# Sample gates in the third mLSTM chunk, their squares one chunk later, and sigmoids ended on ScalarE by Ln and Exp

## What is computed

```
h = _head_rms(jax.nn.sigmoid(_to_heads(o_ml, ML_HEADS)) * h, ml_g)
...
o_h = _head_rms(o_h, hg_g) * jax.nn.silu(_to_heads(hgt, HG_HEADS))
...
mixed = jnp.concatenate([_from_heads(h), _from_heads(o_h)], axis=-1).astype(x.dtype)
out = jnp.einsum('bte,ed->btd', mixed, w_out)
```

## Time and profile before

| | us |
|---|---|
| median of 3 runs | 1206.72 |
| lowest and highest | 1206.54, 1207.07 |
| profiled execution, its own time | 1207.56 |
| its span in the trace | 1205.4 |

### The profile page before, as it was taken

The page is one execution under the profiler, slowest core; times in us unless marked ns, Lnnn a source line. Parts: engine busy times, 40 slices in busy tenths (PEclk is TensorE's granted clock), DMA queues, the critical chain, the costliest instruction groups (busy, mean ns, idle before and its releaser), DMA issues.

```text
span 1205.4 us, 17280 instructions
## 1 busy us (share of the span) xinstructions
PE 1013.3 (84%) x6738; PEld 605.7 (50%) x6738; DVE 600.5 (50%) x1007; ACT 249.1 (21%) x532; POOL 249.1 (21%) x228
## 2 busy tenths in 40 slices
PE   7999999979999696999999999734878899799400
PEld 4666666645656364566656665423434445344100
DVE  1550133347777777797778777362222233231046
ACT  1542111121111122233223322100011111011023
POOL 0000000001110142453344334000000001252165
PEclk9999999989999897999999999855999999899755
DMA  9010101020000243000010001409887779858496
GB/s 386 29 70 1 70 1 70 0 74 1 1 1 1 79 181 158 19 18 18 36 36 18 18 36 53 164 19 369 337 292 289 279 286 339 324 210 318 123 218 179
DMA packets 30681, 154.29 MB, mean 128 GB/s; under 512 B 5546, under 2 KB 5994, under 8 KB 21274
## 3 DMA queue, kind: packets, MB, share of 16 engines
q1 hardware_dynamic: 24938, 130.17, 28.5%
q0 software_dynamic: 5248, 18.94, 6.1%
q10 hardware_dynamic: 432, 4.35, 0.9%
HBM read 321.52 MB, written 23.82 MB: 286 GB/s over the span
## 4 chain that ended last, share of the span: by engine, by line
PE 76%; DMA 11%; DVE 7%; issue 2%; POOL 1%; ACT 1%; SPq 1%; DVEq 0%; ACTq 0%; POOLq 0%
PE psum L1653 17%; PE psum L774 9%; PE psum L1704 9%; PE psum L761 9%; DMA hg_decay<-in_w_up 6%; PE psum L1333 5%; PE psum L1312 4%; PE psum L1328 4%; PE psum L802 4%; DMA x_cm<-y_slots,hg_k 2%; PE psum L736 1%; PE psum L1671 1%; PE psum L1297 1%; POOL x_cm L1423 1%; DMA hg_q<-in_w_down 1%
## 5 line engine op out<-in xcount | busy, mean ns | idle before, releaser
L1653 PE MATMUL psum<-x_cm,weight_slots 128*128 128x344 f32 x720 | 209.0, 453 | 0.0
L1653 PEld LDWEIGHTS psum<-x_cm,weight_slots 128*128 128x128 f32 x720 | 136.6, 190 | 71.9 <-issue 1.1
L1704 PE MATMUL psum<-weight_slots,x_cm 128*128 128x512 f32 x256 | 114.0, 599 | 0.0
L1328 PE MATMUL psum<-weight_slots,scratch 128*32 128x256 f32 x1280 | 80.1, 406 | 23.1 <-DMA weight_slots<-in_w_gate 16.9
L1408 POOL DMA_INDIRECT scratch<-x_rows,hg_k x20 | 19.8, 991 | 307.4 <-PE psum L1297 222.0
L1312 PE MATMUL psum<-conv_qk,scratch 128*32 128x512 f32 x320 | 74.1, 605 | 10.9 <-DMA hg_q<-in_w_down 6.6
L1333 PE MATMUL psum<-conv_qk,scratch 128*32 128x256 f32 x640 | 74.1, 385 | 7.4 <-DMA hg_decay<-in_w_up 7.4
L1704 PEld LDWEIGHTS psum<-weight_slots,x_cm 128*128 128x128 f32 x256 | 48.1, 193 | 54.5 <-issue 54.5
L1333 PE MATMUL psum<-hg_decay,scratch 128*32 128x256 f32 x640 | 74.1, 385 | 0.0
L1312 PE MATMUL psum<-hg_k,scratch 128*32 128x512 f32 x160 | 74.0, 606 | 0.0
L1312 PE MATMUL psum<-hg_q,scratch 128*32 128x512 f32 x160 | 74.0, 606 | 0.0
(11 more groups left out here) (356 smaller groups left out, 1679.5 us busy)
## 6 DMA issues: line engine op xcount, KB each, us to landing
weight_slots<-in_w_gate SPq DMA_DIRECT2D x80, 1024.0 KB
conv_qk<-in_w_up SPq DMA_DIRECT2D x40, 1024.0 KB
hg_decay<-in_w_up SPq DMA_DIRECT2D x40, 1024.0 KB
conv_qk<-in_w_down SPq DMA_DIRECT2D x40, 1024.0 KB
hg_k<-in_w_down SPq DMA_DIRECT2D x20, 1024.0 KB
hg_q<-in_w_down SPq DMA_DIRECT2D x20, 1024.0 KB
weight_slots<-in_w_in SPq DMA_DIRECT2D x6, 2048.0 KB, 7.7
y_slots<-scratch SPq DMA_DIRECT2D x20, 512.0 KB, 7.2
```

Of the source, the lines that this page charges most:

```text
L1328: m = mm(PS[lane, 2, 0:FF], xgT[i][:, k, lane], w_gate[q][:, k], start=(k == 0), stop=(k == KD - 1))
L1653: i = mm(PS[0:m, idx % 4, 0:PIECE], lhs_of(k), xT[:, k, n * PIECE:(n + 1) * PIECE], start=(k == 0), stop=(k == KD - 1))
L1704: i = mm(PS[:, bank, :], xT[:, k, c * P:(c + 1) * P], w_slot(g)[:, k, :], start=(k == 0), stop=(k == KD - 1))
```

## The change

Three things change, and buffers move with them.

1. **Sigmoids.** ACT ends both chunk gates and the samples' gates itself: `exp(-x)`, then `Ln` with a bias of 1, then `Exp` with scale -1, so 1/(1+exp(-x)). The add and the reciprocal on DVE are gone (L1976 and L1977; L1154 and L1155; L674 and L675). In the mLSTM chunk DVE's wait for `o_exp` moves from before the memory update to before the last multiplication.
2. **The samples' gates** run on DVE in the mLSTM chunk c = 2, between the score step and the v step, and not behind the last chunk's output. The two clearing memsets are done by POOL: one behind the mask copy at the start, one behind its last square of the mLSTM loop. The store of the samples' stabiliser (`out_m_s`) moves on SP from stage 3 to between the store of the memory and the load of weight group 7.
3. **The samples' squares** are summed on PE in chunk 1 behind its first level, the root follows on ACT behind `outputs_scale(0)`, `samples_mix` moves from level 2 to 3, the samples' output projection on PE from level 1 to 2, their residual sum on DVE and its root on ACT one level later. Since `squares` now lies in the place of `ln_gb`, SP waits for the sum of squares before it loads `ln_gb`, and the samples' rows of x behind it.

```
-    T = [SC[:, 5632 + n * HB:5632 + (n + 1) * HB] for n in range(24)]
-    squares, both_rstd = SC[:, 6400:6400 + 2 * HB], SC[:, 6464:6464 + 2 * HB]
-    TH = {m: SC[:, 6528 + n * HB:6528 + (n + 1) * HB] for n, m in enumerate((0, 2, 11, 15))}
+    tile32 = lambda at, n=0: SC[:, at + n * HB:at + (n + 1) * HB]
+    squares, both_rstd = SC[:, 8832:8832 + 2 * HB], SC[:, 5696:5696 + 2 * HB]
+    q_dots, decay_args = SC[:, 9216:9216 + 2 * HB], SC[:, 9280:9280 + 3 * HB]
+    T = {0: q_dots[:, 0:HB], 1: q_dots[:, HB:], 8: tile32(9280), 9: tile32(9312), 10: tile32(9344), 6: tile32(9376), 7: tile32(9408),
+         16: tile32(8704), 17: tile32(8736), 15: tile32(5632)}
+    TH = {0: tile32(8768), 2: tile32(8800), 15: tile32(5664), 11: conv_ps[:, 0:HB]}
     T[5], TH[5], T[13], TH[13] = squares[:, 0:HB], squares[:, HB:], both_rstd[:, 0:HB], both_rstd[:, HB:]
-    T[21] = mprev.rearrange("p h c -> p (h c)")[:, 0:HB]
+    T[21] = tile32(9440)
...
+    T[11] = T[12]
...
-    q_apart = [SC[:, 7680:8704], SC[:, 8704:9728]]
+    q_apart = [SC[:, 7680:8704], SC[:, 5632:6656]]
...
         store_v_rows(1)
         sp.wait_ge(s.num_rows, 2)
         sp.dma_start(w_out, t["w_out"].rearrange("(e p) n -> p e n", p=P)).then_inc(s.mixer_in, 16)
-        sp.wait_ge(s.masks_made, 1)
         sp.wait_ge(s.h_turned_read, NCH)
+        sp.wait_ge(s.sq_sum, 1)
+        sp.wait_ge(s.outputs, 16 * outs[0])
         sp.dma_start(ln_gb, t["ln1"].partition_broadcast(P)).then_inc(s.mixer_in, 16)
...
-                out_dma(sp, t["out_m_s"].rearrange("h b -> (h b)").unsqueeze(0), T[21][0:1])
...
@@ -640,11 +644,9 @@
         link(v.tensor_tensor(hb(dec), mb, hb(T[6]), ALU.subtract))
         link(v.tensor_tensor(hb(T[21]), hb(T[6]), lf, ALU.add))
         tell(v.tensor_scalar(nm, T[21], -1.0, None, ALU.mult), s.sgates_arg)
-        dve.wait_ge(s.masks_made, 1)
-        for q in q_apart:
-            link(v.memset(q, 0.0))
         dve.wait_ge(s.qk_silu, 9)
         qs, ks = conv_ps[:, 0:HB], conv_ps[:, HB:2 * HB]
+        dve.wait_ge(s.masks_made, 2)
         link(v.tensor_copy(spread_q(0), hb(qs)))
         link(v.tensor_tensor(T[0], qs, ks, ALU.mult))
         tell(v.tensor_tensor(T[1], qs, n0, ALU.mult), s.dots_in)
@@ -658,6 +660,7 @@
         link(v.tensor_tensor(hb(TH[0]), qS, kS, ALU.mult))
         dve.wait_ge(s.sgates_exp, 2)
         link(v.tensor_tensor(hb(TH[2]), qS, hb(TH[14]), ALU.mult))
+        dve.wait_ge(s.masks_made, 3)
         tell(v.tensor_copy(spread_q(1), hb(TH[2])), s.dots_in)
         link(v.tensor_scalar(dd, dd, KSCALE, None, ALU.mult))
         link(v.tensor_tensor(T[3], ks, dd, ALU.mult))
@@ -668,13 +671,9 @@
 
     def samples_gate(dve, link, kind):
 
-        v = nc.vector
-        gate = (T, TH)[kind][11]
         dve.wait_ge(s.ogate_exp, kind + 1)
-        link(v.tensor_scalar(gate, gate, 1.0, None, ALU.add))
-        link(v.reciprocal(gate, gate))
         if kind == 1:
-            link(v.tensor_tensor(TH[11], TH[11], TH[12], ALU.mult))
+            link(nc.vector.tensor_tensor(TH[11], TH[11], TH[12], ALU.mult))
...
-                    if l == 7:
-                        samples_squares(pe)
-                if c == 1 and l == 1:
+                if c == 1 and l == 0:
+                    samples_squares(pe)
+                if c == 1 and l == 2:
                     project_out_samples()
...
         def gate_exp(kind):
             act.wait_ge(s.zs_read, kind + 1)
-            tell(A((T, TH)[kind][11], (T, TH)[kind][12], ACT.Exp, scale=-1.0), s.ogate_exp)
+            gate = (T, TH)[kind][11]
+            link(A(gate, (T, TH)[kind][12], ACT.Exp, scale=-1.0))
+            link(A(gate, gate, ACT.Ln, bias=one_col))
+            tell(A(gate, gate, ACT.Exp, scale=-1.0), s.ogate_exp)
...
+            if c == 1:
+                norm_scale()
...
-                if l == (3 if c == 1 else 2) and c >= 1:
+                if l == (4 if c == 1 else 2) and c >= 1:
                     ln_scale(ROW_ORDER[c - 1])
...
-                    tell(A(PS[:, 1, :], gtb.rearrange("p h v -> p (h v)"), ACT.Exp, scale=-1.0), s.gt_exp)
+                    link(A(PS[:, 1, :], gtb.rearrange("p h v -> p (h v)"), ACT.Exp, scale=-1.0))
+                    link(A(PS[:, 1, :], PS[:, 1, :], ACT.Ln, bias=one_col))
+                    tell(A(PS[:, 1, :], PS[:, 1, :], ACT.Exp, scale=-1.0), s.gt_exp)
...
-            if c == 0:
-                norm_scale()
...
-                if c == 1 and l == 2:
+                if c == 1 and l == 3:
                     samples_mix(dve, link, tell, 0)
                     samples_mix(dve, link, tell, 1)
-                if l == 2 + late and c >= 1:
+                if l == 2 + 2 * late and c >= 1:
                     residual_sum(ROW_ORDER[c - 1])
...
                     dve.wait_ge(s.gt_exp, c + 1)
-                    link(v.tensor_scalar(PS[:, 1, :], PS[:, 1, :], 1.0, None, ALU.add))
-                    link(v.reciprocal(PS[:, 1, :], PS[:, 1, :]))
                     tell(v.tensor_tensor(gtb, gtb, by_h(PS[:, 1, :]), ALU.mult), s.gt_gated)
...
         out_dma(sp, t["out_C_p"], Cst)
+        sp.wait_ge(s.sgates_arg, 1)
+        out_dma(sp, t["out_m_s"].rearrange("h b -> (h b)").unsqueeze(0), T[21][0:1])
...
                 act.wait_ge(s.o_biased, c + 1)
+                link(A(ogate, ogate, ACT.Exp, scale=-1.0))
+                link(A(ogate, ogate, ACT.Ln, bias=one_col))
                 tell(A(ogate, ogate, ACT.Exp, scale=-1.0), s.o_exp)
...
         tell(nc.gpsimd.tensor_copy(msk[:, :, :].rearrange("p l t -> p (l t)"), mask_words), s.masks_made)
+        nc.gpsimd.memset(q_apart[0], 0.0).then_inc(s.masks_made, 1)
...
+        nc.gpsimd.memset(q_apart[1], 0.0).then_inc(s.masks_made, 1)
...
+            if c == 2:
+                samples_gates(dve, link, tell)
             tell(v.tensor_tensor(vext[c % 2][:, :, 0:P], heads(PS[:, 0, :]), heads(bias[:, 0:512]), ALU.add), s.v_ready)
...
-            dve.wait_ge(s.o_exp, c + 1)
-            link(v.tensor_scalar(ogate, ogate, 1.0, None, ALU.add))
-            link(v.reciprocal(ogate, ogate))
...
+            dve.wait_ge(s.o_exp, c + 1)
             for h in range(H):
                 i = v.scalar_tensor_tensor(hbuf[:, h], PS[:, 4 + h // 2, (h % 2) * DV1:(h % 2) * DV1 + P], rec[:, h:h + 1],
                                            ogate[:, h], ALU.mult, ALU.mult)
             tell(i, s.h_ready)
-            if c == NCH - 1:
-                samples_gates(dve, link, tell)
```

4 lines of the change are left out of this document (2 added, 2 removed).

## The result

The changed kernel takes 1196.53 us (median of 4 runs, 1196.11 to 1198.42), the kernel before 1206.89 us beside it: a ratio of 0.9922, 95% interval 0.9907 to 0.9937. Measured twice more it gave 1196.46 and 1197.17 us (ratios 0.9909 [0.9894, 0.9924] and 0.9914 [0.9898, 0.9930]). The forecast was 1197.0 us, within 1193.8 to 1201.2. The profiled execution took 1196.72 us with a span of 1194.9; that of the kernel before had 1207.56 and 1205.4, so 10.5 us of span are to be accounted for.

The account below looks back on a forecast made before the run. PE bounds the loops; between them, from 404 to 505 us, it stops for DVE. Terms 4.1 + 4.7 + 0.9 = 9.7 us took the median from 1206.72 to 1197.0 us, range 1193.8 to 1201.2.

Parts of the forecast that it names:

- The loops give nothing: mLSTM loop and second to eighth HGRN2 chunk: PE always busy, so cheaper DVE chunks and moved samples' gates change nothing.
- Stop 1: PE's 9.90 us wait ahead of the last transposes: transposes 7.1 us earlier, product 4.4 earlier after weights; carried 4.1 us.
- POOL's memset: Second memset, behind POOL's last square in the mLSTM loop: could hold DVE's scale 0 to 2.3 us, covered by weights.
- the clock: PE's clock at the samples' second product: low again, about the same recovery, 0.3 us worse; low throughout 2.8 worse.
- Stop 2: PE's 9.60 us wait ahead of the samples' squares, end of HGRN2 chunk 0: gate work leaves DVE's chain, 4.7 us gained.
- Stop 3: PE's 1.28 us wait ahead of the samples' projection: goes, less 0.4 for the squares; 0.9 us gained, bounds 0.2 and 1.3.
- Rival A: Layer-norm load late at the samples' projection: PE would wait 5.9 us, gain only 3.8, 1202.9 us; chance 0.08.
- Rival B: Neither PE restart costs clock and the weights land at the short end: up to 12.5 us gained, 1194.2; chance 0.12.
- E: PE's clock stays at 0.50 from the samples' product to 450.4 us: net 20 us slower, 1227; chance 0.05.
- C: ACT late: two passes ahead of level 6 in seven later chunks, 8.7 us lost, 1205.7; chance with F 0.06.
- F: ACT reloads tables at each Ln/Exp switch, so passes end later than DVE, in mLSTM too; chance with C 0.06.
- D: Weight group 7 takes as much longer as it is issued earlier: only 5.6 us gained, 1201.1; chance 0.06.

Follow-up runs that it names:

- the gate's experiment: Changed kernel with only the mLSTM output gate finished by addition and reciprocal on VectorE again: 1202.21 us.
- the gates' place: Changed kernel with only the samples' gates back behind the last mLSTM chunk's h_ready, out_m_s behind weight group 7: 1196.30 us.
- the early group: Changed kernel with SP issuing weight group 7 ahead of its wait for the finished state and the state's store: 1195.10 us.
- the first trace: Profiled execution of the changed kernel in its first comparison with the kernel before, nothing further edited: 1196.72 us, span 1194.9.
- second repeat: The changed kernel measured once more with nothing edited, also called the repeat with the luckier clock: 1197.17 us.

## Why the prediction was right, step by step

**The loops give nothing.** Right in the changed kernel, where TensorE is busy all the time in both. But the samples' gates in the third chunk were called costless on 1.3 us of slack plus what the sigmoid freed. With the sigmoid back, the wait was 0.83 us, about what 1.3 of slack leaves of gates of 2.0: the slack alone doesn't hold them, the freed time does.

**Stop 1, mechanism.** Right, with the numbers. `c_ready` 3.1 us earlier: L1984 started 4.23 us behind its L1766, L1991 1.17 behind L1770, 3.06 less, and 3.1 came back with the gate's experiment. Transposes 7.1 us earlier: 14.52 - 7.51 = 7.0. SP's issue at 407.9 and landing at 416.1 on the old time axis: 405.94 + 1.94 = 407.9, and 416.2. That the weights are late next was shown twice, by the gates' place that costs nothing and by the early group. POOL's memset, bounded at 0 to 2.3 us, took

```profile
408.19 0.95 POOL L1879 MEMSET scratch<- 128x1024 f32 x1
```

in the timeline of POOL, and beside it VectorE's sum L2006 had its usual 0.69 us. That sum has one operand, so the rule that the prediction cites (the Trainium skill, "SBUF — State Buffer", "Who interferes with whom"), on instructions with two SBUF inputs, was not put to the test by the memset. Where POOL's L1005 reads SBUF, VectorE's L1088 with two such inputs took 1.06 instead of 0.42 us (at 446.59, POOL's from 446.38 to 447.37); by that rule it should be held, and the trace agrees.

**Stop 1, size.** The term was 4.1 us. From L1770 to the mixer's first product the change took 22.22 - 19.27 = 2.95 us, and 4.6 in the repeat with the luckier clock. The mis-sized step is the clock: the forecast had the product 0.3 us slower than before (4.47), and it was 6.2, 6.3 and 5.0 us in three traces: 1.4 to 1.5 us beyond that step in the first two, inside its outer bound of 2.8, and 0.2 in the third. The forecast took the clock as low at the transposes and back as fast as before; in the first trace it was still full there, fell in the wait for the weights that the prediction itself had foreseen, and stayed at 0.50 for 5.3 us of the product. That is beyond the 5 us that the prediction had named as a sign of being wrong. Two smaller errors work against each other: the start itself gained 4.1 and not 4.4 us, and the wait of 0.43 us at L609, which the forecast left out, is gone.

**Stop 2,** 4.7 us. The HGRN2 gate was sized at 4.14; putting it back cost 3.8 on the stretch. Level 6 waits 1.99 us for POOL, as foreseen (2.2), ahead of a stop that swallows it. From L760 to L742 the stops 2 and 3 together gave 61.38 - 55.80 = 5.6 us (6.15 in the second repeat); the terms were 4.7 and 0.9. In the first trace 4.3 of them lie ahead of L849 (38.24 us from L761 to L850 before, 33.92 after) and 1.3 behind it: stop 2 was sized 0.4 too high and stop 3 as much too low. The 0.4 are small shifts on VectorE ahead of the heads, among them L1088's 1.06 us.

**Stop 3,** 0.9 us: undoing it cost 1.1 of waits. The mix was done at 469.30 and L783 started at 469.96, 0.7 us of room as the replay had it. Rival A fell: the layer-norm load, issued at 461.39, took

```profile
scratch<-in_ln SPq DMA_DIRECT2D x1, 1024.0 KB, 4.8
```

and was there at 466.2, 3.8 us ahead of L783.

**The sum** of 9.7 us stands against 8.5 in the first trace, 10.8 in the second repeat, and 10.4 to 10.9 in the medians. The first trace's 10.5 us of span came out right partly by luck: 1.9 us were the clock's before the change's place was reached, and 1.4 were lost to it in the product. Rival B (kinder) and E (it stays low) each showed a piece: the clock can be up to 2 us either way, not 20. C and F fell; ScalarE's passes are as long as assumed and nobody waits for them. Groups by line, the mLSTM's three passes and HGRN2's, in PSUM:

```profile
L1860 ACT ACTIVATE scratch<-scratch,constants 128x512 f32<-128x512 f32 x8 | 5.8, 721 | 0.3
...
L964 ACT ACTIVATE psum<-psum,constants 128x512 f32<-128x512 f32 x8 | 5.3, 662 | 0.3
...
L1861 ACT ACTIVATE scratch<-scratch 128x512 f32<-128x512 f32 x8 | 5.0, 630 | 0.3
...
L963 ACT ACTIVATE psum<-scratch 128x512 f32<-128x512 f32 x8 | 4.8, 602 | 20.8 <-DVE scratch L1149 20.8
...
L965 ACT ACTIVATE psum<-psum 128x512 f32<-128x512 f32 x8 | 4.7, 582 | 0.2
```

D (stop 1 gives nothing) fell by the product's start, 4.1 us earlier.

## What to carry to other kernels

Two more passes on an idle ScalarE, in place of an addition and a reciprocal of 3.8 us on VectorE, are worth only as much as another engine waits for VectorE. Here that was so at 2 of 16 places, and the rest of the 65 us saved on VectorE bought nothing. When a stall is taken away, look for what is queued behind the same event: the weight load was tied to the state on SP and took 3 of 7 us back, and a small move that shortens the shorter of two waits shows nothing until the longer one is gone. Small work that nobody needs soon belongs behind the instruction on which the bound engine waits, not ahead of it.
